# Two transformer blocks on one core: convolution factors paired in a PSUM bank, the memory norm's groups re-spaced, the first granule in halves, the last product by token halves

## The reference

```python
# first block (cut)
h = rmsnorm(x, attn_norm_g);  proj = h @ w_in          # 2048 x 9216
...                                                     # spatial gating, attention, w_o, FFN
ple = p @ w_ple
x = x + sigmoid(rmsnorm(x, ple_norm_g) @ w_ple_gate) * ple

# second block (cut)
z = rmsnorm_2(x, g_mix) @ w_in                          # 2048 x 3584
cb, cc, cx, pv, q = split(z, [768, 1536, 2304, 3072])
conv_out = cb * causal_dwconv(cc * cx, conv_w)          # three taps over tokens
pool_out = ...                                          # trailing means of pv, then a small product
kv = rmsnorm_2(mem, g_mem) @ w_kv                       # attention of q on 256 memory rows
x = x + concat([conv_out, pool_out, att]) @ w_out
u = causal_dwconv(rmsnorm_2(x, g_ffn) @ w_up, ffn_conv_w) + ffn_conv_b
x = x + (silu(gate) * val) @ w_down
return rmsnorm_2(x, g_final)
```

## Time and profile before

| | |
|---|---|
| median of 3 runs | 2524.15 us (2521.37 to 2525.26) |
| the profiled execution | 2522.53 us, its span from first to last instruction 2520.4 us |
| TensorE busy | 2491.7 us, 11322 matmuls and transposes |
| VectorE, ScalarE busy | 1402.9 us, 1241.9 us |
| GpSimd busy | 11.0 us, 16 instructions |
| DMA | 473.55 MB, 188 GB/s |
| granted TensorE clock | 0.996 of full, over the span |

### The profile page before, as it was taken

The page is one execution under the profiler, slowest core; times in us unless marked ns, Lnnn a source line. Parts: engine busy times, 40 slices in busy tenths (PEclk is TensorE's granted clock), DMA queues, the critical chain, the costliest instruction groups (busy, mean ns, idle before and its releaser), DMA issues.

```text
span 2520.4 us, 27950 instructions
## 1 busy us (share of the span) xinstructions
PE 2491.7 (99%) x11322; PEld 2069.6 (82%) x11322; DVE 1402.9 (56%) x1666; ACT 1241.9 (49%) x1530; POOL 11.0 (0%) x16
## 2 busy tenths in 40 slices
PE   9999999999999999999999999999999999999998
PEld 7888888888888888888887788888888888888886
DVE  6564555655555554544445654765566665665543
ACT  7454665445444444444444654444555555554443
POOL 0000000000000000000000000000000000000000
PEclk9999999999999999999999999999999999999999
DMA  8666655666666666666666565565666666656663
GB/s 278 184 182 186 194 188 180 188 185 185 190 192 187 189 191 187 190 191 190 190 190 211 161 190 176 163 194 177 185 187 184 183 190 186 186 185 208 195 193 126
DMA packets 131105, 473.55 MB, mean 188 GB/s; under 512 B 14624, under 2 KB 15008, under 8 KB 130720
## 3 DMA queue, kind: packets, MB, share of 16 engines
q1 hardware_dynamic: 130976, 471.77, 61.0%
HBM read 469.61 MB, written 2.10 MB: 187 GB/s over the span
## 4 chain that ended last, share of the span: by engine, by line
PE 97%; DVE 1%; ACT 1%; issue 0%; DMA 0%; SPq 0%; DVEq 0%; ACTq 0%
PE ps L1272 86%; PE ps L1275 8%; PE ps L374 2%; DVE wl L1299 0%; ACT wh L1298 0%; PE ps L732 0%; DVE mg_lo L345 0%; DMA raw<-in_w_in 0%; PE ps L703 0%; PE ps L748 0%; PE ps L580 0%; PE ps L939 0%; PE ps L975 0%; ACT mg_hi L338 0%; DVE X L881 0%
## 5 line engine op out<-in xcount | busy, mean ns | idle before, releaser
L1299 DVE TENSOR_TENSOR wl<-raw,wh 128x1024 fp32r<-128x1024 f32 x878 | 1076.9, 1227 | 1092.7 <-ACT wh L1298 1092.2
L1298 ACT CAST wh<-raw 128x1024 fp32r<-128x1024 f32 x878 | 919.5, 1048 | 1178.0 <-PE ps L1275 1170.9
L1272 PE MATMUL ps<-wh,x1g_hi 128*128 128x512 f32 x704 | 276.3, 392 | 0.0
L1272 PE MATMUL ps<-wh,x4g_hi 128*128 128x512 f32 x704 | 276.2, 392 | 0.0
L1272 PE MATMUL ps<-wh,act_hi 128*128 128x512 f32 x704 | 274.6, 390 | 0.0
L1272 PE MATMUL ps<-wl,x1g_hi 128*128 128x512 f32 x704 | 274.2, 390 | 0.0
L1272 PE MATMUL ps<-wl,x4g_hi 128*128 128x512 f32 x704 | 274.1, 389 | 0.0
L1272 PE MATMUL ps<-wl,act_hi 128*128 128x512 f32 x704 | 274.1, 389 | 0.0
L1272 PE MATMUL ps<-wh,h_hi 128*128 128x512 f32 x576 | 227.8, 395 | 3.3 <-DVE h_lo L454 3.3
L1272 PE MATMUL ps<-wl,h_hi 128*128 128x512 f32 x576 | 224.8, 390 | 0.0
L1272 PE MATMUL ps<-wh,x1g_lo 128*128 128x512 f32 x528 | 205.9, 390 | 0.0
(11 more groups left out here) (267 smaller groups left out, 3163.0 us busy)
## 6 DMA issues: line engine op xcount, KB each, us to landing
raw<-in_w_in SPq DMA_DIRECT2D x200, 512.0 KB, 3.6
raw<-in_w_ffn_in SPq DMA_DIRECT2D x176, 512.0 KB, 3.6
raw<-in_w_up SPq DMA_DIRECT2D x176, 512.0 KB, 4.0
raw<-in_w_ffn_out SPq DMA_DIRECT2D x88, 512.0 KB, 3.5
raw<-in_w_down SPq DMA_DIRECT2D x88, 512.0 KB, 4.2
raw<-in_w_o SPq DMA_DIRECT2D x32, 512.0 KB, 3.6
raw<-in_w_ple_gate SPq DMA_DIRECT2D x32, 512.0 KB, 3.6
raw<-in_w_out SPq DMA_DIRECT2D x32, 512.0 KB, 3.6
```

Of the source, the lines that this page charges most:

```text
L1272: pe.plain(lambda e, a=(dst, lhs, rhs), s=start, p=stop: e.matmul(*a, start=s, stop=p, skip_group_check=True))
L1298: hi = act.do(lambda e, r=r, slot=slot: e.copy(wh[:, r, :], raw[:, slot, :]), in_tok[s], free)
L1299: lo_tok[s] = dve.do(lambda e, r=r, slot=slot: e.tensor_tensor(wl[:, r, :], raw[:, slot, :], wh[:, r, :].bitcast(F32), ALU.subtract), hi)
```

## The change

It has five parts.

1. *Convolution factors.* The columns are laid out as cc0 cx0 cc1 cx1 ... cc5 cx5, then cb0 to cb5. After a turn, cc and cx of one tile lie in the two halves of one PSUM bank. ScalarE copies cc out and VectorE multiplies it by cx straight from PSUM ("u"); the taps (`conv_taps`: the first on ScalarE, two on VectorE) follow one chunk before the cb columns arrive. VectorE multiplies two cb tiles at once from PSUM by two finished taps ("cb"), and `conv_split` splits two tiles at once. GpSimd has no part any more. MIX_ORDER takes pair 6 before pair 2.
2. *Memory norm.* The four groups stand at steps 11, 17, 25 and 30 instead of 13, 16, 19 and 22; the sum of the squares at 34 instead of 26.
3. *First granule.* In step 0 the x pair is split first, then the weights in two halves of 512 columns.
4. *Token halves.* In the last granule of each "N" chunk the six matmuls of the first token half come before those of the second, and the sixth gives a semaphore. Only the last product uses it: each half of X is added as soon as its own sum is ready.
5. *Stores.* In the last block the first half is multiplied by the final gain ahead of the norm; the row scaling is divided differently between VectorE and ScalarE, six stores as before.

```diff
-MIX_ORDER = (12, 14, 0, 2, 6, 8, 10, 4)
+MIX_ORDER = (12, 14, 0, 6, 2, 8, 10, 4)
...
+                    for i, (what, j) in enumerate(uses):
+                        pair = ps[:, 6 + i, :]
+                        if what == "u":
+                            cc = act.do(lambda e, i=i, j=j: e.copy(CW[:, j, :], ps[:, 6 + i, 0:T]), done)
+                            tok = conv_tok[j] = dve.do(lambda e, i=i, j=j: e.tensor_tensor(
+                                CU[:, j, :], CW[:, j, :], ps[:, 6 + i, T:2 * T], ALU.mult), cc)
+                        elif what == "cb":
+                            tok = conv_tok[j] = dve.do(lambda e, i=i, j=j: e.tensor_tensor(
+                                CU[:, j:j + 2, :].rearrange("p k t -> p (k t)"), ps[:, 6 + i, :],
+                                CW[:, j:j + 2, :].rearrange("p k t -> p (k t)"), ALU.mult),
+                                done, conv_tok[j], conv_tok[j + 1])
...
-        for j in range(4):
-            spread(late_at + 9 + 3 * j, j, MR, lambda: got_mats["mr"], "mem", mg, lambda: out1.done, normm)
+        for j, step in enumerate((7, 13, 21, 26)):
+            spread(late_at + step, j, MR, lambda: got_mats["mr"], "mem", mg, lambda: out1.done, normm)
...
+        def conv_taps(step, j):
+            def a():
+                g["o"] = act.do(lambda e: e.activation(CW[:, j, :], CU[:, j, :], ACT.Copy, scale=gain("conv", 12 + j)),
+                                conv_tok[j])
             def b():
+                o = dve.do(lambda e: e.scalar_tensor_tensor(CW[:, j, 1:], CU[:, j, 0:T - 1], gain("conv", 6 + j),
+                                                            CW[:, j, 1:], ALU.mult, ALU.add), g["o"])
+                conv_tok[j] = dve.do(lambda e: e.scalar_tensor_tensor(CW[:, j, 2:], CU[:, j, 0:T - 2], gain("conv", j),
+                                                                      CW[:, j, 2:], ALU.mult, ALU.add), o)
...
+        z_uses = ((("u", 1), ("u", 2)), (("u", 3), ("u", 4)), (("u", 5), ("cb", 0)), (("cb", 2), ("cb", 4)))
         for n in range(4):
+            ch = gemm_chunk(t["w_in2"], "N", x3g, pairs16, after_z(3 + n, z_uses[n], RT, norm4), 3 + n)
+            for i, (what, j) in enumerate(z_uses[n]):
+                if what == "u":
+                    conv_taps(ch.last + RING + 3 + i, j)
+                else:
+                    conv_split(ch.last + RING + 3, j)
+        conv_taps(first_z[2].last + RING + 3, 0)
...
                 tok = [dve.do(lambda e, b=b: e.tensor_tensor(X[:, b, sl], banks(chunk)[b], X[:, b, sl], ALU.add),
-                              chunk.done) for b in range(2)]
+                              (chunk.half, chunk.done)[b]) for b in range(2)]
...
+                gained = dve.do(lambda e: e.tensor_tensor(X[:, 0, sl], X[:, 0, sl], GF[:, sl], ALU.mult), sq[0])
                 rows_root(norm6)
                 rows_invert(norm6)
...
+                by_dve(0, 1536, 2048)
+                by_act(0, 0, 512)
+                by_dve(0, 512, 1536)
+                by_act(1, 0, 1024)
+                store(1, 1536, 2048, dve.do(lambda e: e.scalar_tensor_tensor(
+                    X[:, 1, sl], X[:, 1, sl], RT[:, 1:2], GF[:, sl], ALU.mult, ALU.mult), norm6["tok"]))
+                by_dve(1, 1024, 1536)
...
-                for a in range(2):
+                order = [(a, b) for a in range(2) for b in range(2)]
+                if last:
+                    order.sort(key=lambda ab: ab[1])
+                for a, b in order:
...
+                if stop and chunk.kind == "N":
+                    chunk.half = pe.do(one)
+                else:
+                    pe.plain(one)
...
+            if s == 0:
+                for fn in todo.pop(0):
+                    fn()
+                for c in (slice(0, 512), slice(512, 1024)):
+                    hi = act.do(lambda e, c=c: e.copy(wh[:, 0, c], raw[:, 0, c]), in_tok[0])
+                    lo_tok[0] = dve.do(lambda e, c=c: e.tensor_tensor(
+                        wl[:, 0, c], raw[:, 0, c], wh[:, 0, c].bitcast(F32), ALU.subtract), hi)
```

More of the change, by code:

```diff
@@ L892, in two_block_kernel, with after_z @@
         z_tok = {}
-        def after_z(name, dst, i0, scale, norm, late):
+        conv_tok = {}
+        def after_z(name, uses, scale, norm):
             def after(s, chunk):
@@ L902, in b @@
                     done = rows2_tok["free"] = turn(rows2, g["st"], 6, 4)
[L903 to L908, removed]
+                    z_tok[name] = []
+                    for i, (what, j) in enumerate(uses):
[10 more added lines that the diff above has]
+                        else:
+                            tok = act.do(lambda e, pair=pair, what=what, j=j: e.copy(
+                                what[:, j:j + 2, :].rearrange("p k t -> p (k t)"), pair), done)
+                            z_tok[name].append(tok)
+                        bank_free[6 + i] = tok
+                at(s, a)
+                at(s + 2, b)
             return after
         rows2_tok = {}
-        for j in range(4):
-            spread(late_at + 9 + 3 * j, j, MR, lambda: got_mats["mr"], "mem", mg, lambda: out1.done, normm)
+        for j, step in enumerate((7, 13, 21, 26)):
+            spread(late_at + step, j, MR, lambda: got_mats["mr"], "mem", mg, lambda: out1.done, normm)
         kv_tok = {}
@@ L1073, in conv_tile @@
+                conv_tok[j] = dve.do(lambda e: e.scalar_tensor_tensor(CW[:, j, 2:], CU[:, j, 0:T - 2], gain("conv", j),
+                                                                      CW[:, j, 2:], ALU.mult, ALU.add), o)
             at(step, a)
[L1074 to L1081, removed]
-        for n in range(4):
-            ch = gemm_chunk(t["w_in2"], "N", x3g, pairs16, after_z(3 + n, Z2, 4 * n, RT, norm4, 0), 3 + n)
-            for i, j in enumerate(conv_at[n]):
-                conv_tile(ch.last + RING + 4 + i, j)
+            at(step + 1, b)
@@ new lines, in conv_split, with b @@
+        def conv_split(step, j):
+            g = {}
+            def a():
+                g["hi"] = act.do(lambda e: e.copy(mix.hi[:, j:j + 2, :], CU[:, j:j + 2, :]), conv_tok[j])
+            def b():
+                mix.ready[j] = mix.ready[j + 1] = dve.do(lambda e: e.tensor_tensor(
+                    mix.lo[:, j:j + 2, :], CU[:, j:j + 2, :], mix.hi[:, j:j + 2, :].bitcast(F32), ALU.subtract), g["hi"])
+            at(step, a)
+            at(step + 1, b)
+        z_uses = ((("u", 1), ("u", 2)), (("u", 3), ("u", 4)), (("u", 5), ("cb", 0)), (("cb", 2), ("cb", 4)))
@@ L1197, in after @@
                     return
[L1198 to L1201, removed]
+                sq = [act.do(lambda e, b=b: e.activation(TB[:, 512 * b:512 * b + 512], X[:, b, sl], ACT.Square,
+                                                         accum_out=SUMS[:, b, n:n + 1]), tok[b]) for b in range(2)]
@@ L1202, in after, with by_dve @@
+                norm6["sq"] = sq[1]
+                gained = dve.do(lambda e: e.tensor_tensor(X[:, 0, sl], X[:, 0, sl], GF[:, sl], ALU.mult), sq[0])
                 rows_root(norm6)
                 rows_invert(norm6)
[L1204 to L1214, removed]
+                def by_dve(b, c0, c1):
+                    store(b, c0, c1, dve.do(lambda e: e.tensor_scalar(X[:, b, c0:c1], X[:, b, c0:c1], RT[:, b:b + 1], None,
+                                                                      ALU.mult), norm6["tok"], gained, fin[2]))
@@ L1252, in multiply @@
                     w_lo = wl[:, r, 512 * a:512 * a + 512]
[L1253 to L1259, removed]
+                    x_hi = operand.hi[:, k, b * P:(b + 1) * P]
+                    x_lo = operand.lo[:, k, b * P:(b + 1) * P]
+                    start = first and a == 0
+                    stop = last and a == 1
+                    mms += [(bk[b], x_hi, w_hi, start, False), (bk[b], x_hi, w_lo, False, False),
+                            (bk[b], x_lo, w_hi, False, stop)]
             else:
@@ L1271, in multiply, with one @@
             for dst, lhs, rhs, start, stop in mms[:-1]:
-                pe.plain(lambda e, a=(dst, lhs, rhs), s=start, p=stop: e.matmul(*a, start=s, stop=p,
-                                                                               skip_group_check=True))
+                def one(e, a=(dst, lhs, rhs), s=start, p=stop):
+                    return e.matmul(*a, start=s, stop=p, skip_group_check=True)
+                if stop and chunk.kind == "N":
+                    chunk.half = pe.do(one)
+                else:
+                    pe.plain(one)
             dst, lhs, rhs, start, stop = mms[-1]
```

44 lines of the change are left out of this document (14 added, 30 removed).

## The result

The changed kernel takes 2509.1 us (median of 4 runs, 2508.79 to 2509.36), the kernel before in the same comparison 2522.76 us (4 runs). The ratio is 0.9945, 95% interval 0.9928 to 0.9962: 13.7 us less by the medians. The profiled execution took 2509.36 us, its span 2507.2 against 2520.4: 13.2 us less.

The account below looks back on a forecast made before the run. TensorE, busy for 2491.7 of 2520.4 us, was taken as the bound. Gains of 2.6 (start), 6.4 (gate product), 2.9 (convolution) and 0.9 (tail) sum to 12.8 us; forecast 2510.5 us, own range 2507 to 2514.

Parts of the forecast that it names:

- The start: First granules: TensorE begins 1.2 us earlier and the clock does not fall; gain 2.6 us.
- half subtractions: First granule: VectorE's subtractions on 128x512 halves, taken at 0.7 us each, ending at 7.7 and 8.4.
- The third granule could then start at 14.0: Start: TensorE begins at 8.5 and 5.5 us later reaches the third granule; its last split makes it 14.2.
- Rival 2: Start stays slow: clock falls after the shorter wait, or third granule's weights land later; 1.4 us less gain, 2511.9; chance 0.12.
- The gate product: Gate product and memory norm: respaced groups cut waits and low clock costing 12.3 us to 5.9; gain 6.4 us.
- third turn: Gate product, step 31: the fourth group's mg_lo and fold precede the addition to X; new wait of about 3.4 us.
- Rival 1: Gate product: no pile-up at step 31, VectorE reaches the addition early; 5.7 us more gained, 2504.8; chance 0.12.
- rival 3: Gate product: groups only moved, third turn waits as the first did, clock falls twice; 6.4 us less, 2516.9; chance 0.09.
- the 5.9: Gate product's remaining cost: 0.2 at first turn, 3.4 at third turn, 2.3 for a low clock.
- two to five granules of cover: Convolution: last chunk's split lies that far ahead of use, 5 us or more, so the 2.9 us wait goes.
- The tail: End of the kernel: one square (0.63 us) less and a shorter first stored block; gain 0.9 us.
- rival 4: Every chunk's last granule: splitting costs TensorE a matmul's slot, 23.7 us over 103 chunks, 2534; chance 0.04.

Follow-up runs that it names:

- old start: Changed kernel with the first granule prepared whole and the weights' casts ahead, as before the change; 2509.93 us (one run).
- no halves: Changed kernel without the order by token halves in a chunk's last granule and without the semaphore in its middle; 2510.68 us (one run).
- old order: Changed kernel with the order of the convolution's mixing steps as before, (12, 14, 0, 2, 6, 8, 10, 4); 2510.73 us (one run).
- splits later: Changed kernel with the convolution's splits (hi and lo of the mixing operand) two steps later; 2513.88 us (one run).

## Why the prediction came out as it did

**The start** was mis-sized: 1.96 for 2.6. Its first half held better than asked: TensorE begins at 8.09 behind a wait of 1.34 (8.5 and 2.1 forecast; "half subtractions" taken at 0.7 measure 0.65, and the x pair landed at 4.87 as worked out), and no low clock stands behind it. The step that failed is "The third granule could then start at 14.0": I took the second granule to run on without a stop. It stopped for 0.95 us because the x parts queue behind a cast that waits for the second granule's weights; the run with the x parts first takes that stop away. Rival 2 came in neither of its forms (no fall, no wait for the third granule's weights); it was the second granule's that came late. The other thing is what the gain is made of: two thirds of it (1.3 of 1.96) is a fall of the clock, less a somewhat earlier start, that the execution before had and that the old order, run again, did not. In so far the 1.96 owes to which execution was profiled.

**The gate product** was right in its mechanism: first turn 0.2 forecast and 0.35 measured, third turn 3.4 and 3.43, sum 1.6 (without a fall) and 1.39. Rival 1 (the pile-up does not form) and rival 3 (the third turn waits as the first did, 5.5) fell by the trace; the run with the old places shows that the spacing is the gain. Both sizes were near: the stretch without any wait is 124.72 us, so before paid 13.05 there (12.3 in the prediction) and the changed kernel pays 5.79 (5.9). That the 5.9 is met so closely is luck: it holds 2.3 for a low clock that did not come, and the sum without it was 5.2, short by what each of three waits costs beyond its length. On the clock I was wrong for the profiled execution and mostly right beside it: I expected a fall after the 3.4 us wait; there is none, but four others with the same wait (old start, no halves, old order, splits later) have one. There it costs 0 to 1.2 us in the stretch (130.48 to 131.75 against 130.51), not 2.3, since the sum then waits for nothing.

**The convolution** gained 3.13, the wait of 2.9 and 0.2 behind it. The lead keeps the wait away, as argued, but "two to five granules of cover" was too much. With the mixing order put back, the use comes one granule (2.74) earlier and TensorE waits 0.41, so the slack at that operand is 2.33 us; with the splits two steps later that makes 5.48 - 2.33 = 3.15 us of wait, and 3.14 came. The order of the mixing steps was part of the cover, and I had not priced it.

**The tail** gave 0.89 of 0.9; 0.61 of it goes when the halves go (0.63 in the prediction). The other 0.3 was put down to the shorter first store; no run takes it by itself.

**Halves in every chunk** cost nothing, as the rows had it, and rival 4 is excluded: 0.03 us over 56 chunks.

**The sum**, 12.8 against 13.2 in the profiled pair, is closer than its terms: the start gave 0.6 less, the gate product 0.9 and the convolution 0.2 more.

## What to carry to other kernels

Work that is moved away from a wait has to be followed to the next place where the same engine's queue releases the bottleneck: here the spread of four groups took 5.2 us from one turn and put 3.4 on another, and one group three steps earlier would have taken both. Look for buffers that a moved group shares with what follows (a scratch tile, a bank), not only for its place in the queue. And before a gain is read as cause and effect, ask how much of it is a fall of the clock that stood in one of the two executions.

## What the runs showed that I had not expected

Whether the granted clock falls behind an idle time of TensorE is not settled by the length of that time. It fell to 0.5 to 0.6 (near the 1.2 GHz level) behind 2.71, 2.95, 2.97, 3.14 and 5.5 us, and stayed at 1.00 behind 2.88; at the start it fell behind 3.29 and did not behind 3.08; at the third turn it fell behind 3.43 in four executions and did not in one. Each fall cost 1.6 to 2.3 us where no later wait covered it. It fits that the kernel with more such waits spreads more: 20 executions of the kernel before, run beside the experiments, have spans from 2518.6 to 2523.9 us with mean clocks of 0.994 to 0.997, the five at 0.997 being the five shortest, while the 4 runs of the changed kernel lie within 0.6 us. What decides it in a given execution stays open.
